# Six weight slots of 256 columns for queries, keys and values, in place of four of 384

## The reference

```python
h = rmsnorm(x, g_mix[l])
z = h @ w_in[l]                       # 1024 x 3080
c_b, c_c, c_v, q, k, v, f_logit = jnp.split(z, SPLITS, axis=-1)   # six parts of 512 columns, and 8
q = rmsnorm(q.reshape(B, S, FOX_HEADS, HEAD_DIM), g_q[l])
k = rmsnorm(k.reshape(B, S, FOX_HEADS, HEAD_DIM), g_k[l])
```

## Time and profile before

| | us |
|---|---|
| median of three runs | 1440.4 |
| lowest and highest | 1436.05, 1444.97 |
| the profiled execution, its own time | 1442.33 |
| its span, from first to last instruction | 1440.8 |
| TensorE busy | 1379.3 |
| DVE busy | 1033.5 |
| ACT busy | 832.0 |

### The profile page before, as it was taken

How to read it: one execution, slowest core, us unless ns; L and a number is a source line. 1 busy time by engine, 2 the same in 40 slices (tenths; PEclk the granted TensorE clock), 3 DMA queues, 4 the chain that set the end, 5 groups by cost and what they waited for, 6 DMA issues and landing times.

```text
span 1440.8 us, 19644 instructions
## 1 busy us (share of the span) xinstructions
PE 1379.3 (96%) x7689; PEld 1209.8 (84%) x7689; DVE 1033.5 (72%) x803; ACT 832.0 (58%) x726; POOL 83.2 (6%) x82
## 2 busy tenths in 40 slices
PE   6999989999999999987999999999999999999998
PEld 6897878899989897776888888888888888888786
DVE  4547655645457467556897889888978888889887
ACT  5325354434344434435677777767777778677684
POOL 3100100000001001002000000000000000000400
PEclk9999999999999998997999999999999999999999
DMA  9423243554469423336999999999999899999994
GB/s 304 138 88 118 88 161 132 175 176 165 157 229 355 132 89 118 110 110 220 363 343 408 377 344 397 376 353 388 341 404 385 343 396 383 350 378 346 404 401 177
DMA packets 126628, 386.30 MB, mean 268 GB/s; under 512 B 7938, under 2 KB 61806, under 8 KB 126574
## 3 DMA queue, kind: packets, MB, share of 16 engines
q1 hardware_dynamic: 114686, 365.08, 68.1%
q0 software_dynamic: 3168, 11.54, 2.1%
q10 hardware_dynamic: 8720, 8.91, 1.7%
HBM read 369.78 MB, written 15.73 MB: 268 GB/s over the span
## 4 chain that ended last, share of the span: by engine, by line
PE 75%; DVE 10%; ACT 5%; DMA 5%; issue 4%; SPq 0%; POOL 0%; ACTq 0%; DVEq 0%
PE bank L1501 40%; PE bank L1497 16%; PE bank L1498 16%; DVE wl L1055 4%; DMA ring<-in_we_down 3%; ACT wh L735 2%; DVE wl L1036 2%; DMA ring<-in_we_gate 2%; PE bank L1923 1%; ACT wh L721 1%; DVE xl L1061 1%; DVE scratch L1184 1%; DVE scratch L1167 1%; DMA ring<-in_w_in 0%; ACT xh L939 0%
## 5 line engine op out<-in xcount | busy, mean ns | idle before, releaser
L1055 DVE TENSOR_TENSOR wl<-ring,wh 128x2816 fp32r<-128x2816 f32 (+1 forms) x127 | 400.3, 3171 | 62.7 <-PE bank L1501 40.5
L735 ACT ACTIVATE wh<-ring 128x2816 fp32r<-128x2816 f32 (+1 forms) x128 | 336.9, 2632 | 126.1 <-DMA ring<-in_we_down 43.0
L1036 DVE TENSOR_TENSOR wl<-ring,wh 128x3072 fp32r<-128x3072 f32 (+2 forms) x65 | 185.9, 2859 | 115.5 <-ACT wh L721 106.2
L1497 PE MATMUL bank<-wh,xh 128*128 128x512 f32 x528 | 200.6, 380 | 11.1 <-DVE wl L1055 6.6
L1055 DVE TENSOR_TENSOR wl<-ring,wh_third 128x2816 fp32r<-128x2816 f32 (+1 forms) x64 | 187.0, 2923 | 31.5 <-PE bank L1501 29.0
L1498 PE MATMUL bank<-wh,xl 128*128 128x512 f32 x528 | 199.1, 377 | 0.0
L1501 PE MATMUL bank<-wl,xh 128*128 128x512 f32 (+1 forms) x768 | 194.8, 375 | 0.0
L721 ACT ACTIVATE wh<-ring 128x3072 fp32r<-128x3072 f32 (+1 forms) x64 | 151.4, 2366 | 73.9 <-PE bank L1498 42.5
L735 ACT ACTIVATE wh_third<-ring 128x2816 fp32r<-128x2816 f32 (+1 forms) x64 | 155.5, 2430 | 43.2 <-DMA ring<-in_we_up 19.5
L1501 PEld LDWEIGHTS bank<-wl,xh 128*128 128x128 f32 x768 | 141.7, 188 | 18.4
L1497 PE MATMUL bank<-wh,ah 128*128 128x512 f32 x328 | 128.7, 392 | 1.7 <-DVE wl L1036 1.7
(11 more groups left out here) (273 smaller groups left out, 2092.6 us busy)
## 6 DMA issues: line engine op xcount, KB each, us to landing
ring<-in_we_gate SPq DMA_DIRECT2D x64, 1408.0 KB, 7.4
ring<-in_we_up SPq DMA_DIRECT2D x64, 1408.0 KB, 7.8
ring<-in_we_down SPq DMA_DIRECT2D x56, 1536.0 KB, 8.8
ring<-in_w_in SPq DMA_DIRECT2D x16, 1536.0 KB, 9.7
ring<-in_w_gate SPq DMA_DIRECT2D x6, 1536.0 KB, 6.6
ring<-in_w_up SPq DMA_DIRECT2D x6, 1536.0 KB, 6.6
ring<-in_w_down SPq DMA_DIRECT2D x6, 1536.0 KB, 6.4
rows_of<-zeros ACTq DMA_DIRECT2D x1, 8704.0 KB, 43.8
```

The lines of the kernel that those rows point to most:

```text
L735: nc.scalar.activation(wh_in_pass(j, n), ring[:, slot, 0:n], ACT.Copy).then_inc(high_ready, 1)
L1036: nc.vector.tensor_tensor(wl[:, j, 0:n], ring[:, slot, 0:n], wh[:, j, 0:n].bitcast(F32), ALU.subtract).then_inc(low_ready, 1)
L1055: nc.vector.tensor_tensor(wl[:, j % 2, 0:n], ring[:, j % NSLOT, 0:n], wh_in_pass(j, n).bitcast(F32), ALU.subtract).then_inc(low_ready, 1)
L1497: nc.tensor.matmul(dst, x_high, w_high, start=first, stop=False)
```

## The change

The 1536 columns of queries, keys and values come in six slots of 256 columns, each 128 x 2048 elements for ACT and DVE: one for each of `qk0` to `qk3`, and two for the values. The convolution keeps four slots of 384 columns, numbered 6 to 9. `high` of slots 2 to 5 stands at i = 0, 1, 2, 3 of ACT's loop. On DVE `low` of slots 2, 4 and 5 stands at i = 0, 2, 3 directly behind the copy, and `low` of slot 3 at i = 1 behind `erow`, ahead of the memory's copies. A value token tile is made in two halves of 256 columns, where there was one of 128 and one of 384. The number of products stays as it is.

```diff
     for l in range(L):
-        for s in range(8):
-            add_fill((l, "z", s), z_src(l, (3 * CC + ZCOLS * s) if s < 4 else ZCOLS * (s - 4)), (KT, ZCOLS))
+        for s in range(6):
+            add_fill((l, "z", s), z_src(l, 3 * CC + 256 * s, 256), (KT, 256))
+        for s in range(4):
+            add_fill((l, "z", 6 + s), z_src(l, ZCOLS * s, ZCOLS), (KT, ZCOLS))
...
-        for s, n in ((1, "qk2"), (3, "v1"), (5, "conv2"), (7, "conv5")):
+        for s, n in ((0, "qk0"), (1, "qk1"), (2, "qk2"), (3, "qk3"), (5, "v1"), (7, "conv2"), (9, "conv5")):
             frees[l, "z", s] = n
...
                     square(l, f"qk{i}", sq[:, 2 * i:2 * i + 2, :], zqk[:, 2 * i:2 * i + 2, :])
-                    if i in (0, 2):
-                        high_of(l, "z", 2 + i // 2)
+                    high_of(l, "z", 2 + i)
...
-                    if i in (1, 2):
-                        low_of(l, "z", 1 + i)
+                    if i != 1:
+                        low_of(l, "z", 2 + i)
...
                         nc.vector.tensor_scalar(erow[:], erow[:], EPS, None, ALU.mult).then_inc(erow_ready, 1)
+                        low_of(l, "z", 3)
                         if l == 0:
...
-                        channel_tile(ps[:, (c % 2) * S:(c % 2) * S + S], (l, "z", c // 3), ZCOLS, (c % 3) * P, c % 3 == 2,
+                        channel_tile(ps[:, (c % 2) * S:(c % 2) * S + S], (l, "z", c // 2), 256, (c % 2) * P, c % 2 == 1,
                                      done(l, f"qk{i}") if c % 2 else None)
...
-                for t in range(TT):
-                    token_tile(open_bank(l, f"v{t}")[:, 0:P], (l, "z", 2), ZCOLS, 2 * P, 3 * P, t, t == TT - 1, None)
-                for t in range(TT):
-                    token_tile(bank(l, f"v{t}")[:, P:4 * P], (l, "z", 3), ZCOLS, 0, 3 * P, t, t == TT - 1, done(l, f"v{t}"))
+                for s in range(2):
+                    for t in range(TT):
+                        ps = open_bank(l, f"v{t}") if s == 0 else bank(l, f"v{t}")
+                        token_tile(ps[:, 256 * s:256 * s + 256], (l, "z", 4 + s), 256, 0, 256, t, t == TT - 1,
+                                   done(l, f"v{t}") if s else None)
```

More of the change, by code:

```diff
@@ L148, in add_fill, with z_src @@
         fills.append((src, shape))
-    def z_src(l, c0):
-        return w_in[l][:, c0:c0 + ZCOLS].rearrange("(k p) c -> p k c", p=P)
+    def z_src(l, c0, n):
+        return w_in[l][:, c0:c0 + n].rearrange("(k p) c -> p k c", p=P)
     for l in range(L):
-        for s in range(8):
-            add_fill((l, "z", s), z_src(l, (3 * CC + ZCOLS * s) if s < 4 else ZCOLS * (s - 4)), (KT, ZCOLS))
+        for s in range(6):
+            add_fill((l, "z", s), z_src(l, 3 * CC + 256 * s, 256), (KT, 256))
+        for s in range(4):
+            add_fill((l, "z", 6 + s), z_src(l, ZCOLS * s, ZCOLS), (KT, ZCOLS))
         for s in range(4):
@@ L800, in _ @@
                         nc.scalar.activation(crow[:, P:3 * P], fz[:, 0, :], ACT.Copy).then_inc(chigh_ready, 1)
-                high_of(l, "z", 4)
+                high_of(l, "z", 6)
                 for i in range(2):
@@ L806, in _ @@
                                          ).then_inc(take(l, f"v{i}"), 1)
-                high_of(l, "z", 5)
+                high_of(l, "z", 7)
                 guess_rows(l, "qk", "ssqk", mqk[:], 0.0)
@@ L813, in _ @@
                     if i in (0, 2):
-                        high_of(l, "z", 6 + i // 2)
+                        high_of(l, "z", 8 + i // 2)
                 high_of(l, "xkv", 0)
@@ L1144, in _ @@
                         ins.then_inc(decay_ready, 1)
-                low_of(l, "z", 4, 5)
+                low_of(l, "z", 6, 7)
                 refine_rows(l, "qk", "ssqk", mqk[:], 0.0)
-                low_of(l, "z", 6)
+                low_of(l, "z", 8)
                 for i in range(4):
@@ L1152, in _ @@
                                                    ALU.mult, ALU.mult).then_inc(take(l, f"bq{i}"), 1)
-                low_of(l, "z", 7)
+                low_of(l, "z", 9)
                 for i in range(2):
@@ L1658, in _ @@
                     for c in (2 * i, 2 * i + 1):
-                        channel_tile(ps[:, (c % 2) * S:(c % 2) * S + S], (l, "z", 4 + c // 3), ZCOLS, (c % 3) * P, c % 3 == 2,
+                        channel_tile(ps[:, (c % 2) * S:(c % 2) * S + S], (l, "z", 6 + c // 3), ZCOLS, (c % 3) * P, c % 3 == 2,
                                      done(l, f"conv{i}") if c % 2 else None)
```

## The result

The changed kernel takes 1432.5 us (median of six runs, 1429.77 to 1435.49), the kernel before 1440.6 us over its own six. The ratio is 0.9946, with a 95% interval from 0.9929 to 0.9963: 8 us less, where 10.3 were forecast. Five more rounds of the same kernel, beside nineteen runs of the one before, gave 1431.6 us and 0.9935 (0.992 to 0.995), 9 us less.

The account below looks back on a forecast made before the run. TensorE, busy 1379.3 of 1440.8 us, was taken to bound the kernel. Gains of 8.7 us in layer 0 and 1.6 in layer 1, 10.3 together, off the 1440.4 median gave 1430.1 us; range 1426 to 1434, wider 1423 to 1440.

Parts of the forecast that it names:

- the half clock behind the wait for `f`: Layer 0, `qk2` and `qk3`: products at full clock instead of 1.2 GHz at first, 11.5 us for 14.3, gain 2.8.
- First slot: Layer 0, up to `qk1`: the 2.58 us wait goes, products run at full clock, `qk1` done 4.0 us earlier.
- The walk: Step-by-step timing of ACT, DVE and TensorE through the projection; bank to `low` takes 5.5 us against 5.76 of products.
- Opening of `qk2`: Layer 0: `low` of slot 2 moves ahead, so `qk2` opens at 33.1, 6.4 us earlier than 39.51.
- The clock behind the waits: Layer 0: the 1.2 GHz level behind waits for the first slot and `f`, costing 1.8 and 2.8 us.
- New waits in layer 0: TensorE waits for conversions that must follow their banks: 0, 1.9 and 0.9 us for slots 3, 4 and 5.
- The values: Value products, both layers: regrouped into equal 256-column halves, 11.5 us against 13.8, 2.3 us less per layer.
- rival that narrow products are not the cost: Value products, both layers: the new grouping gains nothing, so the kernel takes 1434.7 us; chance 0.04.
- Layer 1: Projection: 1.1 us from shorter `low`, 2.3 from values, less waits of 1.1 and 0.7: gain 1.6 us.
- Behind the stages: Everything after the projections keeps its instructions and order and moves ahead by the summed gain, 10.3 us.
- the rival of the half clock behind a new wait: A new wait in each layer brings the half clock back, 2.8 us per fall: 1435.7 us; chance 0.18.
- The slower case: Conversions fall behind at slots 3 to 5, both layers, with half clock: 32 us more, 1462; chance 0.04.

Follow-up runs that it names:

- the order alone: The kernel before, its 384-column slots kept, with only `low` of slot 2 moved behind the copy of `qk0`: 1439.7 us, ratio 0.9984.

## Why the prediction was right, point by point

The forecast of 1430.1 us lies 2.4 us from the measured median, inside the range, and the sign is right. The mechanism is right too, but that the number lies so close is in part luck: the terms missed by -0.4 to +1.4 us each, and the stages of the first profile gained over 1 us more than their sum, while the half clock behind the wait for `f`, booked at 2.8 us, is there in one profile of two.

- **First slot.** Expected: products from 18.5, `qk1` done at 30.3. The products start at 18.01, `low` runs from 15.66 as walked out, and DVE copies `qk1` at 29.8. Right, half a microsecond short: the forget products ended sooner, at the higher clock for their first and last microsecond. The walk names two waits of TensorE and passes over a third, 2.77 us ahead of the forget products, which stays and has slow products behind it in both kernels. `high` began at 13.67 without waiting for the landing, which does not tell a landing at 12.9 from one at 13.6.
- **Opening of `qk2`.** Expected 33.1, with 0.6 us of wait; it was 31.74, with none. The memory was scaled 1.5 us sooner than I walked out (L1014 at 22.74, not 24.2). The landing did not set it, ACT took the memory as soon as it was free. ACT's part is 2.9 us (22.27 to 19.35), where the walk booked 2.4 although its own terms, 1.06 and two times 0.84, give 2.7. The other 1.05 us is GpSimd's step, which ended with DVE's `low` in the kernel before; the walk had no term for that. The cause that I named, `low` of slot 2 between `qk1` and the step that takes `f`, is shown by putting it back: 1.92 us of wait. That the move needs the narrower slot is shown by the order alone, which gained 0.9 us.
- **The clock behind the waits.** This is the term that was taken for surer than it is. I booked 2.8 us for the half clock behind the wait at 39.51. The second profile of the kernel before has the wait and not the half clock. The other one, behind the wait for the first slot, came in both. So the stage of layer 0 gave 9.8 us against one profile and 7.4 against the other, where 8.7 were expected; at the forget biases it is 8.3 and 7.3. That may be why the timed gain of 8 to 9 us is less than 10.3, but the timed runs have no traces that would show it.
- **New waits in layer 0.** Expected 0, 1.9 and 0.9 us for slots 3, 4 and 5. Measured 0, 1.97 and 0.36. The walk through DVE was right, the memory's copies included; what it lacked is GpSimd's hold on DVE, which cost 0.5 us ahead of slot 4, while DVE's steps ahead of it came 0.4 us sooner behind the opening of `qk2`. That 1.9 was met so closely is these two together.
- **The values.** Expected 11.5 us, measured 57.74 - 45.46 - 0.36 = 11.9, against 13.8 before: a gain of 1.9 us, not 2.3, in both layers. The rival that narrow products are not the cost fell with the products of 128 columns at 0.11 us.
- **Layer 1.** Expected 1.6 us. The first 1.1 came as worked out, and so did the wait of 1.15 us for slot 3; the 0.7 for slot 5 did not, because TensorE reached the end of slot 4 as its `low` ended (455.77 + 2.29 = 458.06, products from 458.12). That leaves 1.1 + 1.9 - 1.15 = 1.8 us. From the transposes to `ssqk` the profiles took 48.0 and 46.9 us before and 45.2 and 43.9 after, 3 us less on average. The rest is the clock, which was at 0.50 there for 6.8 and 3.4 us before, and for 3.4 and 0 after.
- **Behind the stages.** That everything behind "moves ahead by that" is right only on average. The expert passes took 788.2 and 793.1 us in two profiles of the same kernel.
- **The rivals.** The wait of 1.97 us did not bring the half clock, in two profiles of two. But with `low` of slot 2 put back a wait of 1.92 us did, and in layer 1 the wait for the splitting, 2.17 us in every profile of the changed kernel and its variants, was followed by it in five of nine, the first one among them. So the rival of the half clock behind a new wait was not refuted; that it stayed out is in part luck. The slower case did not come near.

What stays open is what in the execution decides whether a wait of 2 to 3 us is followed by the half clock; no run here was made to tell that.

## What to carry to other kernels

Let a slot of weights end where the bank that uses it ends. Then the engines that prepare the next slot are released one bank earlier, and only with that did moving their instructions bring more than 1 us here. Before moving an instruction, look at who waits for it on every engine, GpSimd too: what it sets free may collide with the instructions it was to make room for, and an instruction that takes several times its usual length is the sign. And take a second profile of the unchanged kernel before giving a cause to a few microseconds far from the edit.

## What the runs showed of the hardware

- A product of 128 moving columns costs TensorE nearly as much as one of 256: 0.11 us against 0.12 at the 2.4 GHz level, and 0.18 for 384. At the 1.2 GHz level both take 0.21.
- During a long series of products of 128 columns the clock fell to the 1.2 GHz level and stayed there for about 20 us, with TensorE busy throughout; 2 us before the fall it had waited 1.96 us. That was in layer 0 of one profile, and not in layer 1 of the same one.
- A GpSimd multiplication of 2048 elements per partition stretched a 0.41 us step of DVE to 3.83 us and was itself stretched from 3.61 to 5.70. In the kernel before, a GpSimd step of 0.25 us that began during a `low` took 1.30 us and ended with it.
- One wait of 3.0 us was followed by the half clock in one profile and not in the other, in the same kernel at the same place. One of 2.17 us was in five profiles of nine. In the two stages, from the first slot of layer 0 on, all other waits of 2.5 us and more came with it, and none of 1.15 us did.
- The view of the granted clock can give 1.00 where the products are at the lower level: in the kernel before, from 13.4 to 17.9 us, products of 256 columns start 0.21 us apart at a granted clock of 1.00. The spacing has to be read beside it.
